# S5 part in compact form: 16-channel coefficients, products on 64x64 quadrants, moves of U, kernel and result through memory

## What is computed

```python
uf = u.reshape(bn, l, S5_GROUPS, S5_CH)           # 16 groups of 16 channels
bu_re = jnp.einsum('blgc,gpc->blgp', uf, bb_re)   # 64 complex states a group
...                                               # scan over time, s = a*s + bu
y = (jnp.einsum('blgp,gcp->blgc', s_re, c_re) - jnp.einsum('blgp,gcp->blgc', s_im, c_im)
     + uf * d_skip)
y = jax.nn.gelu(y.reshape(bn, l, BRANCH))
y = y * jax.nn.sigmoid(jnp.einsum('blc,cn->bln', y, w_glu))
```

## Time and profile before

| | us |
|---|---|
| median of 3 runs (351.09, 351.1, 353.65) | 351.1 |
| the profiled execution's own time | 353.67 |
| its span, first to last instruction | 351.8 |
| PE busy in the span | 330.3 |
| DVE busy | 236.1 |
| ACT busy | 121.0 |

### The profile page before, as it was taken

One profiled execution on the slowest core, in us unless ns is written; L12 is line 12 of the kernel. 1 busy time (PEld: TensorE's weight loads), 2 busy tenths in 40 slices (PEclk: granted clock), 3 DMA queues, 4 the chain that ended last, 5 costly groups with the idle time before them and its releaser, 6 DMA issues.

```text
span 351.8 us, 6392 instructions
## 1 busy us (share of the span) xinstructions
PE 330.3 (94%) x2546; PEld 280.9 (80%) x2546; DVE 236.1 (67%) x501; ACT 121.0 (34%) x262; POOL 43.4 (12%) x81
## 2 busy tenths in 40 slices
PE   7899998889999999989979999999999999989991
PEld 6688876667889898869967888887888989877990
DVE  2574499986628978485749727596644897686454
ACT  4243001150691003583412620115177010566321
POOL 4018530006000000250000000000600000120000
PEclk9999999999999999899999999999999999999997
DMA  8977622232531500799915472322262242476503
GB/s 281 380 258 229 241 95 86 61 109 72 163 111 61 180 2 2 240 199 273 351 39 159 141 268 91 119 80 102 92 182 64 102 136 66 124 192 120 184 1 123
DMA packets 28013, 50.85 MB, mean 145 GB/s; under 512 B 6288, under 2 KB 6864, under 8 KB 27984
## 3 DMA queue, kind: packets, MB, share of 16 engines
q1 hardware_dynamic: 25968, 44.06, 37.9%
q0 software_dynamic: 1728, 6.29, 7.5%
q10 hardware_dynamic: 288, 0.09, 0.1%
HBM read 46.80 MB, written 3.64 MB: 143 GB/s over the span
## 4 chain that ended last, share of the span: by engine, by line
PE 75%; DVE 13%; POOL 4%; ACT 4%; issue 2%; DMA 1%; DVEq 0%; POOLq 0%; ACTq 0%
PE pr L490 41%; PE pr L764 10%; DVE att L1327 2%; PE wk L557 2%; DVE h L1059 2%; PE wk L679 2%; PE wk L504 2%; PE wk L725 2%; POOL lev L1577 2%; PE wk L602 1%; POOL lev L1579 1%; PE wk L570 1%; DMA x<-in_xt 1%; PE wk L671 1%; PE wk L617 1%
## 5 line engine op out<-in xcount | busy, mean ns | idle before, releaser
L490 PE MATMUL pr<-h,wring 128*128 128x264 f32 x768 | 178.9, 389 | 3.2 <-DVE h L1059 3.2
L490 PEld LDWEIGHTS pr<-h,wring 128*128 128x128 f32 x768 | 143.3, 190 | 30.0 <-issue 5.9
L764 PE MATMUL pr<-a_hi,w_hi 128*128 128x264 f32 x96 | 27.6, 288 | 0.0
L764 PE MATMUL pr<-a_lo,w_hi 128*128 128x264 f32 x96 | 27.2, 283 | 0.0
L764 PE MATMUL pr<-a_hi,w_lo 128*128 128x264 f32 x96 | 27.2, 283 | 0.0
L877 ACT ACTIVATE v<-pr 128x264 f32<-128x264 f32 x12 | 4.7, 388 | 48.2 <-PE pr L490 48.2
L865 ACT ACTIVATE h<-x 128x264 f32<-128x264 f32 x24 | 9.5, 420 | 32.8 <-DVE x L1480 30.7
L948 ACT ACTIVATE zs<-pr 128x264 f32<-128x264 f32 x16 | 6.0, 384 | 41.7 <-PE pr L490 41.7
L1327 DVE COPY_PREDICATED att<-masks,wk 128x512 f32<-128x512 int32 x20 | 17.6, 950 | 1.0
L764 PEld LDWEIGHTS pr<-a_lo,w_hi 128*128 128x128 f32 x96 | 18.1, 188 | 0.1
L764 PEld LDWEIGHTS pr<-a_hi,w_hi 128*128 128x128 f32 x96 | 18.1, 188 | 0.1
(11 more groups left out here) (281 smaller groups left out, 539.6 us busy)
## 6 DMA issues: line engine op xcount, KB each, us to landing
wring<-in_w_in SPq DMA_DIRECT2D x100, 256.0 KB, 3.0
wring<-in_w_out SPq DMA_DIRECT2D x20, 256.0 KB, 3.7
w_hi<-in_w_out POOLq DMA_DIRECT2D x6, 512.0 KB, 4.3
w_lo<-in_w_out POOLq DMA_DIRECT2D x6, 512.0 KB, 7.8
x<-in_xt SPq DMA_DIRECT2D x2, 528.0 KB, 4.7
out_y<-h SPq DMA_DIRECT2D x4, 264.0 KB, 2.0
s5m_t<-in_s5m SPq DMA_DIRECT2D x2, 512.0 KB, 4.4
ss<-in_hg_in SPq DMA_DIRECT2D x2, 512.0 KB, 4.0
```

The lines of the kernel that those rows point to most:

```text
L490: mm = nc.tensor.matmul(ring_bank(layer, i)[:, 0:TT], wring[:, slot, n, :], act_in[:, k, :], start=(k == 0), stop=(k == KT - 1))
L764: mm = nc.tensor.matmul(ring_bank(layer, i)[:, 0:TT], w[:, j % WSLOTS, n, :], a[:, k, :], start=(k == 0 and p == 0), stop=(k == KT - 1 and ...
```

## The change

The coefficients keep 16 channel columns a state (`GC`) instead of 32: `s5m_t`, `bb`, `ca` are half as wide, and a pair's two groups differ by the half of the partitions they stand on. SP loads `s5m_t` in 8 transfers a layer instead of one (`s5_matrices`), for layer 0 behind chunk 5 and for layer 1 behind output tile 5. PE multiplies each group by itself, on the quadrant (rows 64g, columns 64g) of the array. The kernel within a block goes from DVE to `resp`, with the skip weights added on its diagonal, and by 8 transfers into `tmat` (`block_kernel`), now 64 wide. U is taken out of PSUM sorted by the token's place in its block (`s5_in_rows`), stored to memory (`u_rows`) and loaded into `ub` by 8 transfers (`u_to_rows`); Y goes to memory by 10 transfers and from there to `yg` by one (`y_from_rows`), all issued by SP. `s5_relay` and `s5_back` are gone. `yg` keeps the sorted order and twice the value; `s5_mix` puts both right (4 DVE instructions instead of 2).

```diff
-        s5m_t = sb("s5m_t", 4, S5T, 32)
+        s5m_t = sb("s5m_t", 4, S5T, GC)
...
-        tmat = sb("tmat", S5T, P)
+        bb_re, bb_im, bb_t = (lev[:, i * 512:i * 512 + 512].rearrange("p (s j c) -> p s j c", s=S5T, j=SL) for i in range(3))
+        ca_re = sb("ca_re", S5T, NPW, GC)
+        ca_im = sb("ca_im", S5T, NPW, GC)
+        tmat = sb("tmat", S5T, SL * GC)
+        resp = sb("resp", S5T, SL * GC)
...
+        u_rows = nc.dram_tensor("u_rows", [DEPTH, 2 * P, TT], F32, kind="Internal").ap()
+        y_rows = nc.dram_tensor("y_rows", [DEPTH, 2 * P, TT], F32, kind="Internal").ap()
...
+            def s5_matrices(layer):
+                for g in range(2):
+                    rows = slice(64 * g, 64 * g + 64)
+                    for i in range(4):
+                        sp.dma_start(s5m_t[rows, i, :, :], s5m[layer, rows, i, :, GC * g:GC * g + GC]).then_inc(s5m_in, 16)
+            def u_to_rows(layer):
+                sp.wait_ge(chunk_evac, layer * NCH + C_U1 + 1)
+                sp.dma_start(u_rows[layer].rearrange("(t p) x -> p t x", p=P), u[:, :, :]).then_inc(u_out, 16)
+                if layer == 0:
+                    sp.wait_ge(set_ready, 1)
+                sp.wait_ge(u_out, 16 * (layer + 1))
+                for g in range(2):
+                    rows = u_rows[layer].rearrange("(s g c) x -> g c s x", g=2, c=GC)[g]
+                    for q, (src, to) in enumerate(((slice(192, 264), slice(0, NS + SC)), (slice(64, 128), slice(NS, NS + SC)),
+                                                   (slice(0, 64), slice(NS, NS + SC)), (slice(128, 200), slice(NS, NS + SC + NS)))):
+                        at = 64 * g + GC * q
+                        sp.dma_start(ub[at:at + GC, :, to], rows[:, :, src]).then_inc(u_in, 16)
+            def block_kernel(layer):
+                sp.wait_ge(resp_ready, layer + 1)
+                for g in range(2):
+                    for q in range(SL):
+                        at = 64 * g + GC * q
+                        sp.dma_start(tmat[at:at + GC, :, GC * (3 - q):], resp[64 * g:64 * g + GC, :, 0:GC * (q + 1)]).then_inc(tmat_in, 16)
+            def y_from_rows(layer):
+                sp.wait_ge(yb_ready, layer + 1)
+                yv = yb.rearrange("p (s k) -> p s k", s=S5T)
+                for g in range(2):
+                    rows = y_rows[layer].rearrange("(s g c) x -> g c s x", g=2, c=GC)[g]
+                    for j in range(SL):
+                        at = 64 * g + GC * j
+                        sp.dma_start(rows[:, :, SC * j:SC * j + SC], yv[at:at + GC, :, 0:SC]).then_inc(y_out_rows, 16)
+                    sp.dma_start(rows[:, :, TP:TT], yv[64 * g:64 * g + GC, :, SC:]).then_inc(y_out_rows, 16)
+                sp.wait_ge(y_out_rows, 16 * 10 * (layer + 1))
+                sp.dma_start(yg[:, :, :], y_rows[layer].rearrange("(t p) x -> p t x", p=P)).then_inc(yg_in, 16)
...
                     chunk(w_in[layer, i])
+                    if i == NCH - 3:
+                        u_to_rows(layer)
+                    if i == NCH - 1:
+                        block_kernel(layer)
...
+                        s5_matrices(0)
+                        for g in range(2):
+                            at = 64 * g + GC * g
+                            sp.dma_start(skip_w[64 * g:64 * g + GC, :], par_d[at:at + GC, Q_S5D:Q_S5D + LS]).then_inc(skip_in, 16)
                         sp.dma_start(s5i[:, :, :, :, :], s5_in).then_inc(small_in, 16)
...
-                    if i == 3 and layer + 1 < DEPTH:
+                    if i == 3:
+                        y_from_rows(layer)
+                    if i == 5 and layer + 1 < DEPTH:
                         sp.wait_ge(glu_done, layer + 1)
-                        sp.dma_start(s5m_t[:, :, :, :], s5m[layer + 1]).then_inc(s5m_in, 16)
+                        s5_matrices(layer + 1)
                     if i == 4:
                         sp.wait_ge(s5f_ready, layer + 1)
...
+                for n, src in enumerate((bb_re, bb_im)):
+                    for s in range(S5T):
+                        for g in range(2):
+                            rows = slice(64 * g, 64 * g + 64)
+                            mm = nc.tensor.matmul(wk[rows, n, 64 * s:64 * s + 64], src[rows, s, :, :].rearrange("p j c -> p (j c)"),
+                                                  c("ident")[rows, rows], start=True, stop=True)
...
                 pe.wait_ge(tr_evac, layer * 6 + 6)
...
+                for s in range(S5T):
+                    for n, (b, ca) in enumerate(((bb_re, ca_re), (bb_im, ca_im))):
+                        for g in range(2):
+                            rows = slice(64 * g, 64 * g + 64)
+                            mm = nc.tensor.matmul(wk[64 * g:64 * g + GC, 4, 64 * s:64 * s + 64], b[rows, s, 0, :],
+                                                  ca[rows, s, 0:SL, :].rearrange("p j c -> p (j c)"),
+                                                  start=(n == 0), stop=(n == 1), skip_group_check=True)
                 mm.then_inc(kt_done, 1)
...
-                pe.wait_ge(u_ready, layer + 1)
-                pe.wait_ge(gtr_evac, layer * 4 + 4)
+                pe.wait_ge(u_in, 16 * 8 * (layer + 1))
+                pe.wait_ge(gtr_evac, layer * 2 + 2)
                 for n in range(2):
                     for s in range(S5T):
                         a = (NS + SC) * (s % 4)
...
+                        for g in range(2):
+                            rows = slice(64 * g, 64 * g + 64)
+                            mm = nc.tensor.matmul(wk[rows, 2 * n + s // 4, a:a + NS + SC], gtr[rows, n, s, :], ub[rows, s, 0:NS + SC],
+                                                  start=True, stop=True)
                 mm.then_inc(s5v_done, 1)
...
                 if n:
                     pe.wait_ge(y_evac, layer * 2 + 1)
                 for s in range(4 * n, 4 * n + 4):
...
+                    a = 72 * (s - 4 * n)
+                    parts = ((tmat[:, s, :], ub[:, s, NS:]), (ca_re[:, s, 1:NPW, :].rearrange("p j c -> p (j c)"), sr[:, s, :]),
+                             (ca_im[:, s, 1:NPW, :].rearrange("p j c -> p (j c)"), si[:, s, :]))
+                    for k, (w, data) in enumerate(parts):
+                        for g in range(2):
+                            rows = slice(64 * g, 64 * g + 64)
+                            mm = nc.tensor.matmul(wk[rows, 4, a:a + 72], w[rows], data[rows], start=(k == 0), stop=(k == 2),
+                                                  skip_group_check=True)
                 mm.then_inc(y_done, 1)
...
-                pe.wait_ge(yg_ready, layer + 1)
-                pe.wait_ge(yg_act, layer + 1)
+                pe.wait_ge(yg_in, 16 * (layer + 1))
                 pe.wait_ge(wg_in, 16 * (layer + 1))
...
-            def s5_relay(layer):
...
-            def s5_back(layer, groups):
...
+            def s5_in_rows(layer, i, t):
+                act.wait_ge(proj_done, layer * NCH + i + 1)
+                src = ring_bank(layer, i)[:, 0:TP].rearrange("p (k j) -> p j k", j=SL)
+                step(fn(u[:, t, 0:2 * SC].rearrange("p (j k) -> p j k", j=2), src[:, 1:3, :], ACT.Copy))
+                step(fn(u[:, t, 2 * SC:3 * SC], src[:, 0, :], ACT.Copy))
+                step(fn(u[:, t, 3 * SC:3 * SC + NS], ring_bank(layer, i)[:, TP:TT], ACT.Copy))
+                step(fn(u[:, t, 3 * SC + NS:TT], src[:, 3, :], ACT.Copy), chunk_evac)
...
-                evac(layer, C_U1, u[:, 1, :])
-                s5_relay(layer)
+                s5_in_rows(layer, C_U1, 1)
...
                     silu(layer, i)
...
+                if layer == 0:
+                    dve.wait_ge(skip_in, 32)
+                for g in range(2):
+                    rows = slice(64 * g, 64 * g + GC)
+                    step(tt(skip[rows], c("ident")[rows, rows].unsqueeze(1).to_broadcast([GC, S5T, GC]),
+                            skip_w[rows, S5T * layer:S5T * layer + S5T].unsqueeze(2).to_broadcast([GC, S5T, GC]), ALU.mult))
+                    step(cp(resp[rows, :, :].rearrange("p s m -> p (s m)"), wk[rows, 4, :]))
+                settle()
+                for g in range(2):
+                    rows = slice(64 * g, 64 * g + GC)
+                    step(tt(resp[rows, :, 0:GC], resp[rows, :, 0:GC], skip[rows], ALU.add), resp_ready if g else None)
...
-            def s5_back(layer, groups):
...
             def s5_mix(layer):
-                dve.wait_ge(yg_act, layer + 1)
+                dve.wait_ge(yg_in, 16 * (layer + 1))
                 dve.wait_ge(glu_tanh, layer + 1)
                 step(stt(out=glu[:, :, :], in0=glu[:, :, :], scalar=1.0, in1=yg[:, :, :], op0=ALU.add, op1=ALU.mult))
                 settle()
                 for t in range(2):
-                    step(stt(out=zs[:, t, :], in0=glu[:, t, :], scalar=0.5, in1=zs[:, t, :], op0=ALU.mult, op1=ALU.mult), mix_ready)
+                    z = zs[:, t, 0:TP].rearrange("p (k j) -> p k j", j=SL)
```

(31 more changed lines are left out.)

87 lines of the change are left out of this document (20 added, 67 removed).

## The result

| | median us | runs | profiled execution | span | mean granted clock |
|---|---|---|---|---|---|
| before | 351.1 | 350.23 to 353.65 | 353.67 | 351.8 | 0.990 |
| after | 357.91 | 355.97 to 360.45 | 360.45 | 358.7 | 0.966 |

The ratio after/before is 1.0178, with a 95% interval of 1.012 to 1.0235: slower by 1.8%. The forecast (350.0, range 344.0 to 356.5) had the wrong sign, and the range did not hold the result. Rival B, at 356.5, is the nearest.

The account below looks back on a forecast made before the run. PE was taken as the bound (94% busy, 75% of the chain of waits). From the median, 351.1 -3.9 (coefficients) -6.7 (quadrants) +6.0 (Y's way) +3.4 (clock) = 349.9; forecast 350.0 us, range 344.0 to 356.5.

Parts of the forecast that it names:

- Rival B: Y's load queues behind POOL's `w_hi` loads, PE waits 6 us a layer, clock low longer: 356.5 us; chance 0.15.
- Step 1: Half the coefficients on DVE: PE's three waits for `qe` in layer 0 go, gain 3.86 us, bounds 1.65 and 3.9.
- D: Rival: layer 0's waits for `qe` don't go, another stands just behind: 352.8 us; chance 0.10.
- Step 2: S5 products on PE's quadrants: 33 ns a pass, 9.5 us a layer instead of 12.85, gain 6.7 in both.
- T: End of the second half of Y's products on PE, from which the prediction counts Y's way to the gate.
- C: Rival: quadrant products don't overlap, since both write the same PSUM bank, +10.0 instead of -6.7: 366.6 us; chance 0.05.
- Step 3: Moves of U, the block kernel and the coefficients by SP's transfers stay hidden behind PE's work: priced at nothing.
- Step 4: Y through memory before the gate: PE stands 3.0 us a layer, loss 6.0 in both; bounds 0.7 and 6.6.
- Step 5: Clock at the gate: lower level expected in both layers after tiny products and standing; a fall costs some 1.7 us.
- no change: Forecast of 350.0 us, within the 1% (3.5 us) a measurement can tell, leaning to faster; within 1% given 0.44.
- A: Rival: Y's detour hides nearly whole, PE waits 1 us or less, clock holds: 342.5 us; chance 0.25.

Follow-up runs that it names:

- experiment 6: Changed kernel with the four sums of `sample_states` put behind the gelu on DVE: 357.52 us, ratio 1.0107 to the kernel before.
- experiment 4: Changed kernel with twelve useless products of 264 columns on PE ahead of the gate: 355.11 us, ratio 1.0066 to the kernel before.
- experiment 1: Changed kernel without Y's ten stores and load, gate and mix reading what stands in `yg`: 342.65 us, ratio 0.9707 to the kernel before.
- experiment 8: Changed kernel with chunk 24 and `ret_means` before the gate, sums behind the gelu, half the stores on ACT's queue, `w_hi` released earlier: 349.83 us, ratio 0.9913.
- experiment 9: As experiment 8, with ACT's three negated copies of `w_hi` ahead of the gate's tanh: 341.96 us, ratio 0.9742 to the kernel before.
- experiment 11: Kernel before, with chunk 24 and `ret_means` ahead of the gate and ACT's negated copies ahead of its tanh: 353.92 us, ratio 1.0007.
- experiment 5: Changed kernel with chunk 24 and `ret_means` put ahead of the gate on PE: 359.05 us, ratio 1.0165 to the kernel before.
- experiment 10: As experiment 5, with ACT's negated copies of `w_hi` ahead of the gate's tanh: 347.8 us, ratio 0.9891 to the kernel before.
- experiment 2: Changed kernel with POOL's three `w_hi` loads held back until Y's load has landed: 357.6 us, ratio 1.0108 to the kernel before.

## Why the prediction was wrong

**Step 1, right.** One instruction of `s5_c` takes 0.82 us and one of `s5_b` 0.69 (forecast 0.84 and 0.71). All three waits for `qe` are gone, `s5_turn` starts 4.3 us earlier against 3.9. The fourth wait (0.58, for ACT) stayed, as said. D falls.

**Step 2, right.** 31 ns a pass (2.01 us for 64) where I took 33; from `s5_turn` to T each layer gained 3.36 us where I had 3.35. C falls: diagonal quadrants wrote one bank at 30 to 34 ns a pass, where C charged 62. A chunk's pass of 264 moving columns takes 235 ns (16 in 3.76), so 72 columns alone would be 64 by that rate, an estimate: neighbours overlapped. My own 62 was scaled wrongly, by moving columns, though L557 has 72 of them already; only C's price hung on it.

**Step 3, right but for SP's queue.** PE waited for neither `ub` nor `tmat`, and no wait of it is put down to a weight chunk. But the eight moves of the kernel took 0.77 us each on SP, not 0.45; timelines of SP and of DVE:

```profile
104.28 6.15 SPq L446 DMA_DIRECT2D tmat<-resp  x8
...
111.63 6.29 SPq L416 DMA_DIRECT2D qm<-sample_values  x12
```

```profile
119.62 2.29 DVE L1425 TENSOR_TENSOR qm<-qm,k 128x2048 f32<-128x2048 f32 x1 [1.30 <-DMA qm<-sample_values]
```

`s5_inputs`, which these loads of `sample_values` wait for, ended at 107.57, but SP came to them at 111.63. I had allowed "a microsecond late, with an edge only in step 4". It was 1.3 late (0.7 in layer 1), and that edge is the first part of step 4's error: `yb_ready` came at T + 5.2 and T + 4.6, not T + 4.2.

**Step 4, the step that failed.** The wait was put at 3.0 us a layer, with bounds of 0.7 and 6.6; it was 5.86 and 7.99, the second beyond the bound. In both layers together that is 13.8 instead of 6.0; the time missed by 7.9.

| from T (124.37 and 293.58), us | forecast | layer 0 | layer 1 |
|---|---|---|---|
| gelu done | 4.2 | 5.2 | 4.6 |
| to the start of the last issue | 4.1 | 4.2 | 5.2 |
| the last store lands | 1.9 | 4.7 | 6.1 |
| the load | 3.5 | 2.6 | 2.8 |
| together, with the semaphores | 14.0 | 16.7 | 18.9 |

PE's own work of 11.0 us was right (10.9). The term that was missized is the landing of the small stores, 7.0 us too little in the two layers. I took it from a store that ran alone (1.9), and for the upper bound from `sample_values` (3.0), while giving the neighbourhood of `w_hi` only to the load; in neither bound did the stores pay for it. That was an error of method. The stores start at T + 5 and end at T + 10; `w_hi` is released by PE's own products at about T + 8. That they meet could be read from the order of the work. The sum over both legs, 4.4 alone, is much the same whichever leg it hits: 7.3 and 8.95 here, where the stores paid, and 7.6 in layer 0 of experiment 6, where the load did.

**Step 5, right in the level, too small in the price.** The clock was at 0.50 at both gates. Against the profiled execution that cost 3.6 us, twice the 1.7 of the sum, because each fall is dearer than before: 2.8 and 2.5 us (experiment 4) against 1.7. In the kernel before the clock falls inside the gate (0.73 on average in the window from 143 to 144, then 0.50); here it is low from the gate's first pass, since it fell in the stand. That the stand is its only cause is not right, as the trace without Y's way shows. What all traces have in common is what PE did before the gate. Tiny products and then a stand: low in ten layers of ten. Tiny products and no stand: low in two of four (the kernel before, the second trace of experiment 1). Chunk 24 or fillers and no stand over 1.1 us: low in none of eight (experiments 4, 8, 9, 11). Chunk 24 and then a stand of 1.9 to 3.8 us: a slower gate in two of four (2.82 and 3.17 us, experiments 5 and 10).

**The forecast of "no change".** Two gains of 3.9 and 6.7 were right to some tenths (4.3 and 6.7), so it was not luck that steps 1 and 2 came out; the sum failed on step 4 and, by some 2 us, on step 5.

**Rivals.** B named the place, the neighbour and the size (PE waits 6 us, clock 4), and both came out. Its condition (over 13 us from `yb_ready`) was met in layer 1, 298.19 to 312.39, and not in layer 0, where 11.5 us (129.54 to 141.04) were enough, because `yb_ready` itself was 1.0 late. In the changed kernel it was wrong in which leg waits: the load took 2.6 and 2.8 us, not 5, and the stores 4.7 and 6.1, not 3. A's price was right for a kernel whose way for Y is covered: 342.5, ratio 0.9755, against 0.9707 without the way and 0.9742 in experiment 9. Only the covering had to be written.

## What to carry to other kernels

A way through memory is priced with what else the transfer engines do in that stretch, and both its legs pay: put the release of each bulk load of the neighbourhood on the same time line as the small stores and the load behind them. A stand that opens is best filled with the engine's own later work, but then look at the second engine's queue behind the same point: experiment 5 gained nothing, and experiment 10, with one line moved on ACT, is 2.7% better by the ratios. A slower result may be a good change in a wrong order; here a kernel without Y's way showed how much there was to win.

## What had not been expected of the hardware

The very start differs between executions. The first 16 products (the mean of squares of the input, the only thing on PE then) took 6.2 us in the two profiled executions of before and after, and 3.8 in three others, with 647 ns against 386 ns as the median of one. These are the durations that the gate's products have at 0.50 and at 1.00, though the windows name 1.00 in either case there, so that it is the clock is read from the durations alone. Chains of the changed kernel and of experiment 2:

```profile
5.34 6.25 PE wk L561 x16
```

```profile
5.30 3.84 PE wk L561 x16
```

Everything behind it moves by 2.4 us. In the profiled executions, experiment 1's first left out, the group took from 3.84 to 6.52 us. Besides, seven of the thirteen traces have a stretch of about 3 us at 0.50 behind the norm between the layers, between 174 and 187 us, and the others don't (those of before and after among them): 16 products then took 5.3 instead of 3.8 us. Together that is 4 us, and the 17 runs of before beside experiments 9 and 10 lie between 350.6 and 356.94. Whether these two make the whole scatter was not tried. It is why the ratios above, and not single profiled executions, carry the conclusions on time.

The issue of a small transfer on SP's queue was 0.43 us for most shapes, 0.60 at the least for the moves of the kernel between two places on chip (1.5 at the most), and one of the stores in layer 1 held the queue for 1.47 us while `w_hi`'s loads were being issued. These loads are not the reason, for experiment 2 has the same at the store before it, 7 us ahead of them (chain, layer 1):

```profile
296.58 1.60 SPq L456
```
